# A hybrid DiT layer on one core: latents normalised tile by tile, gate rows loaded ahead of the down weights, router scaling split between ACT and GpSimd

## The reference, cut to what matters

```python
mod = silu(cond) @ w_ada + b_ada               # shift1, scale1, gate1, shift2, scale2, gate2
h   = rmsnorm(x, norm1) * (1 + scale1) + shift1
proj = h @ w_in                                # conv gates and values, cq 256, ckv 128, k_rope 32, merge gates
q   = rmsnorm(cq, q_norm) @ w_uq               # 8 heads x 96, 32 of them rotated
kv  = [rmsnorm(ckv, kv_norm), cache] @ w_ukv   # 8 heads x (64 + 64)
x   = x + gate1 * ((sig(g_conv) * conv + sig(g_mla) * attention) @ w_mix_out)
h2  = rmsnorm(x, norm2) * (1 + scale2) + shift2
route(h2 @ w_grp, h2 @ w_exp)                  # best of 4 groups, best 2 of its 8 experts
x   = x + gate2 * sum over experts(combine * (silu(h2 @ w_gate) * (h2 @ w_up)) @ w_down)
y   = rmsnorm(x, final_norm)
```

## Time and profile before

| | us |
|---|---|
| median of 3 runs (971.71 to 972.36) | 971.86 |
| the profiled execution, its own time | 970.25 |
| its span, first to last instruction | 968.4 |
| PE busy | 883.6 (91% of the span) |
| DVE, ACT, POOL busy | 411.7, 275.2, 106.6 |
| HBM traffic | 214 GB/s over the span |

### The profile page before, as it was taken

The page is one execution under the profiler, slowest core; times in us unless marked ns, Lnnn a source line. Parts: engine busy times, 40 slices in busy tenths (PEclk is TensorE's granted clock), DMA queues, the critical chain, the costliest instruction groups (busy, mean ns, idle before and its releaser), DMA issues.

```text
span 968.4 us, 14912 instructions
## 1 busy us (share of the span) xinstructions
PE 883.6 (91%) x6004; PEld 694.5 (72%) x6004; DVE 411.7 (43%) x854; ACT 275.2 (28%) x499; POOL 106.6 (11%) x121
## 2 busy tenths in 40 slices
PE   3698888999989999999999999994699999999886
PEld 2487546888789999999999997883355555555441
DVE  1437345444425234351521284568244334443232
ACT  5334835444421311212122132342011111111122
POOL 0000000000000000000000031001122332333220
PEclk9799998999999999999999999996799999999999
DMA  8951593112112122212222232797999999999938
GB/s 339 364 206 67 191 337 100 31 61 65 64 58 79 52 87 87 81 49 87 87 88 87 66 131 60 233 321 279 373 397 408 405 407 405 407 404 401 397 129 325
DMA packets 83919, 198.83 MB, mean 205 GB/s; under 512 B 11384, under 2 KB 43112, under 8 KB 83608
## 3 DMA queue, kind: packets, MB, share of 16 engines
q1 hardware_dynamic: 76040, 181.71, 51.0%
q0 software_dynamic: 7824, 16.36, 4.5%
HBM read 189.30 MB, written 18.17 MB: 214 GB/s over the span
## 4 chain that ended last, share of the span: by engine, by line
PE 79%; DMA 9%; DVE 4%; ACT 3%; SPq 3%; issue 1%; DVEq 0%; POOLq 0%; ACTq 0%
PE pair L798 12%; PE pair L1284 11%; PE pair L1288 11%; PE pair L1286 11%; PE pair L817 6%; PE pair L1277 5%; PE pair L1279 5%; PE pair L1278 5%; PE pair L1424 3%; PE pair L786 2%; DMA w_ug<-in_w_gate 2%; PE pair L1446 2%; PE pair L1436 2%; DMA ada_b<-in_w_ada 2%; DMA ya<-expert_rows 1%; DMA gate<-mod_rows 1%
## 5 line engine op out<-in xcount | busy, mean ns | idle before, releaser
L798 PE MATMUL pair<-w_ug,xgT 128*64 128x256 f32 x1184 | 141.9, 394 | 6.6 <-DMA w_ug<-in_w_gate 5.8
L1616 ACT CAST hi<-raw 128x2048 fp32r<-128x2048 f32 (+3 forms) x36 | 63.3, 1757 | 231.1 <-PE pair L1288 202.1
L1793 DVE TENSOR_TENSOR lo<-raw,hi 128x2048 fp32r<-128x2048 f32 (+3 forms) x36 | 78.5, 2181 | 118.5 <-ACT hi L1616 118.0
L798 PEld LDWEIGHTS pair<-w_ug,xgT 128*64 128x64 f32 x1184 | 85.4, 141 | 49.9 <-issue 8.2
L1288 PE MATMUL pair<-hT,lo 128*128 128x320 f32 x512 | 116.7, 309 | 0.0
L1284 PE MATMUL pair<-hT,hi 128*128 128x320 f32 x512 | 116.7, 309 | 0.0
L1286 PE MATMUL pair<-hT,hi 128*128 128x320 f32 x512 | 116.6, 309 | 0.0
L1284 PEld LDWEIGHTS pair<-hT,hi 128*128 128x128 f32 x512 | 85.6, 188 | 0.2 <-issue 0.2
L1288 PEld LDWEIGHTS pair<-hT,lo 128*128 128x128 f32 x512 | 85.6, 188 | 0.0
L1286 PEld LDWEIGHTS pair<-hT,hi 128*128 128x128 f32 x512 | 85.5, 188 | 0.0
L934 ACT ACTIVATE sa<-pair 64x256 f32<-64x256 f32 x37 | 14.1, 380 | 209.5 <-PE pair L798 209.5
(11 more groups left out here) (325 smaller groups left out, 1403.7 us busy)
## 6 DMA issues: line engine op xcount, KB each, us to landing
w_ug<-in_w_up SPq DMA_DIRECT2D x32, 1024.0 KB
w_ug<-in_w_gate SPq DMA_DIRECT2D x32, 1024.0 KB
w_dn<-in_w_down SPq DMA_DIRECT2D x32, 1024.0 KB
raw<-in_w_in SPq DMA_DIRECT2D x20, 1024.0 KB, 5.2
ada_a<-in_w_ada SPq DMA_DIRECT2D x16, 1024.0 KB, 10.0
ada_b<-in_w_ada SPq DMA_DIRECT2D x8, 1024.0 KB, 11.1
ya<-expert_rows SPq DMA_DIRECT2D x5, 1024.0 KB, 9.0
raw<-in_w_conv_out SPq DMA_DIRECT2D x4, 1024.0 KB, 5.0
```

The costliest lines, as they stand in the source:

```text
L798: x = pe.matmul(bank[2 + d % 2][g * SL:(g + 1) * SL, 0:DE], xgT[d % 2][:, k, h * SL:(h + 1) * SL], w_ug[r][:, g, h, k, :], start=(n == 0), ...
L1616: act.copy(hi[n % 2][:, 0:size], raw[n % 4][:, 0:size]).then_inc(hi_done, 1)
L1793: dve.tensor_sub(lo[n % 2][:, 0:size], raw[n % 4][:, 0:size], hi[n % 2][:, 0:size].bitcast(F32)).then_inc(lo_done, 1)
```

## The change

There are three groups of edits.

1. Latent stage. Roots and reciprocals are taken tile by tile, each tile with its own count (`s_rmsl`, `s_latn`), and PE transposes a tile after the count of that tile alone. Of the modulation pieces only 8 to 11 stay ahead of the transposes; 12 goes between the fourth and fifth tile, 13 to 15 between the key products (`ADA_KV`), all in bank 6. Pieces 14 and 15 load into `raw[0]` and `raw[1]`. The transposes go to banks 5, 0, 1, 2, 3, 4 with the rotary keys of the first four tiles in bank 7, the queries to (5, 0) and (1, 2), and `q_turn` has a single pair of banks (3, 4): each one now waits until ACT has copied the one before (`s_tqe`). Both halves of the `w_ukv` split stand later: DVE's behind the last query tile, ACT's behind the six rotary-key copies.
2. Last mix quarter and router. The +1 on scale2 is taken when the vector is made; the product with norm2 (1,024 columns for each stream) moves from one DVE instruction to two on GpSimd. `row_shift(3)` stands ahead of `add_y(1, 4)`. The four latent tiles' logits are scaled by ACT, in four small instructions behind the last `lg_out`, and DVE adds the shift to all four at once.
3. Gate rows. `gate2` lies elsewhere in SBUF; its four loads are issued as soon as the h2 rows are made, ahead of the downs of experts 1 and 2; DVE waits for them in step 1 only, where it first uses them.

```diff
 # SP
         sp.wait_ge(s_h2g, NT)
+        for st in range(2):
+            for h in range(2):
+                sp.dma_start(gate2[h * SL:(h + 1) * SL, st, :].rearrange("p (g c) -> p g c", g=2),
+                             MODW[3].rearrange("(g r) c -> g r c", g=4)[2 * h:2 * h + 2, st].partition_broadcast(SL)
+                             ).then_inc(s_g2, 16)
         sp.wait_ge(s_lg, NT)
...
         rows_stored(sp)
-        for st in range(2):
-            for h in range(2):
-                sp.dma_start(gate2[...
...
+                if q >= 14:
+                    sp.wait_ge(lo_done, q - 13)
+                    sp.wait_ge(ada_used, q - 5)
+                elif q == 13:
+                    sp.wait_ge(ada_used, 12)
+                elif q >= 6:
                     sp.wait_ge(ada_used, q - 5)
...
-        for q in range(12, N_ADA):
+        for q in (12, 14, 15, 13, *range(N_ADA2, N_ADA)):
             ada(q)
             if q == 19:
+                sp.wait_ge(ada_used, N_ADA2)
 # GpSimd
+        pool.wait_ge(s_n2, 48)
+        for st in range(2):
+            pool.tensor_mul(gain2[:, st, :], gain2[:, st, :], norm2_b[:, :]).then_inc(s_n2, 1)
 # ACT
+    def lg_scale(act, i):
+        act.wait_ge(s_lgT, i + 1)
+        act.wait_ge(s_h2g, i + 1)
+        act.activation(lg[:, i, :], lgT_of(i), ACT.Copy, scale=stat[:, 64 + i:65 + i]).then_inc(s_lge, 1)
...
         lg_out(act, NT - 1)
+        for i in range(NTS):
+            lg_scale(act, i)
...
-        for r, n in ((RQ, QL), (RKV, KVL)):
-            x = act.activation(stat[:, r:r + NT], stat[:, r:r + NT], ACT.Sqrt, scale=1.0 / n, bias=stat[:, 95:96])
-        x.then_inc(s_rmsl, 1)
-        act.wait_ge(s_ukv_v, 16)
-        split_hi(N_UKV, NH * P)
+            for r, n in ((RQ, QL), (RKV, KVL)):
+                x = act.activation(stat[:, r + i:r + i + 1], stat[:, r + i:r + i + 1], ACT.Sqrt, scale=1.0 / n,
+                                   bias=stat[:, 95:96])
+            x.then_inc(s_rmsl, 1)
 # PE
-        for q in range(N_ADA1, N_ADA2):
-            ada(q, bank[4 + q // 4][:, 0:256])
-        pe.wait_ge(s_latn, NT)
+        for q in range(N_ADA1, 12):
+            ada(q, bank[6][:, 0:256])
         for i in range(NT + 1):
...
+            if i == NTS:
+                pe.wait_ge(s_mod, 3)
+                ada(12, bank[6][:, 0:256])
+            if i < NT:
+                pe.wait_ge(s_latn, i + 1)
...
         def q_turn(i):
             pe.wait_ge(s_qr, i + 1)
-            if i < 2:
-                pe.wait_ge(s_kr, 2 * i + 4)
-            if i >= 2:
-                pe.wait_ge(s_tqe, i - 1)
+            if i == 0:
+                pe.wait_ge(s_lTe, NT + 1)
+                pe.wait_ge(s_kr, 4)
+            else:
+                pe.wait_ge(s_tqe, i)
...
+                if j in ADA_KV:
+                    ada(ADA_KV[j], bank[6][:, 0:256])
 # DVE
-        dve.wait_ge(s_rmsl, 1)
-        dve.reciprocal(stat[:, 32:37], stat[:, RQ:RQ + NT])
-        link(dve.reciprocal(stat[:, 37:42], stat[:, RKV:RKV + NT]))
         for i in range(NT):
             b = bank[i]
+            dve.wait_ge(s_rmsl, i + 1)
+            dve.reciprocal(stat[:, 32 + i:33 + i], stat[:, RQ + i:RQ + i + 1])
+            link(dve.reciprocal(stat[:, 37 + i:38 + i], stat[:, RKV + i:RKV + i + 1]))
...
-        dve.wait_ge(s_n2, 48)
-        link(dve.scalar_tensor_tensor(out=gain2[:, :, :], in0=gain2[:, :, :], scalar=1.0,
...
         row_gain(3)
+        row_shift(3)
         add_y(1, NT - 1)
-        row_shift(3)
         row_gain(4)
-        dve.wait_ge(s_lgT, 4)
-        for i in range(NT - 1):
-            lg_rows(i)
         row_shift(4)
+        dve.wait_ge(s_lge, NT + NTS)
+        link(dve.tensor_add(lg[:, 0:NTS, :], lg[:, 0:NTS, :], shift_bc[:, 0:1, :].to_broadcast([P, NTS, NG + NE])))
         dve.wait_ge(s_lgT, NT)
-        lg_rows(NT - 1)
+        lg_rows(NTS)
...
+            if isinstance(j0, int) and d == 1:
+                dve.wait_ge(s_g2, 64)
...
-        dve.wait_ge(s_g2, 64)
```

More of the change, by code:

```diff
@@ L412, in both, with kr_ps @@
         return pair[p][:, :].rearrange("p (h c) -> p h c", h=2)[:, :, 0:HALF]
+    def kr_ps(i):
+        if i < NTS:
+            return bank[7][0:ROPE, i * P:(i + 1) * P]
+        return bank[4][0:ROPE, 0:P] if i == NTS else bank[4][0:ROPE, 384:512]
     w_in = io["w_in"][0]
@@ L416, in build @@
     kcol = [0, 128, 256, 384, 640, 512]
+    lat_bank = [5, 0, 1, 2, 3, 4]
+    q_bank = [(5, 0), (1, 2)]
+    turn_bank = (3, 4)
+    kv_bank = (0, 1, 2, 5)
+    KR_ORDER = (0, 1, 4, 5, 2, 3)
+    ADA_KV = {1: 13, 3: 14, 5: 15}
     stream = [0, 0, 0, 0, 1]
@@ L443, in ada_buf @@
         if q < N_ADA2:
-            return ada_a[q % 6], ada_a_in[q % 6], 16 * (q // 6 + 1)
+            place = {13: ada_a[5], 14: v3(raw[0], 2, D), 15: v3(raw[1], 2, D)}.get(q, ada_a[q % 6])
+            return place, ada_a_in[q % 6], 16 * (q // 6 + 1)
         return ada_b[q % 4], ada_b_in[q % 4], 16 * ((q - N_ADA2) // 4 + 1)
@@ L1368, in q_of @@
         def q_of(i):
-            pe.wait_ge(s_lTe, i + 1)
-            if i == 1:
-                pe.wait_ge(s_kr, 2)
+            pe.wait_ge(s_lTe, 2 * i + 2 if i < 2 else i + 1)
             if i >= 2:
@@ L1381, in q_turn @@
             pe.wait_ge(s_qr, i + 1)
-            if i < 2:
-                pe.wait_ge(s_kr, 2 * i + 4)
-            if i >= 2:
-                pe.wait_ge(s_tqe, i - 1)
+            if i == 0:
+                pe.wait_ge(s_lTe, NT + 1)
+                pe.wait_ge(s_kr, 4)
+            else:
+                pe.wait_ge(s_tqe, i)
             for h in range(NH):
-                x = pe.transpose(bank[4 + 2 * (i % 2) + h // 4][0:QK, (h % 4) * P:(h % 4 + 1) * P],
+                x = pe.transpose(bank[turn_bank[h // 4]][0:QK, (h % 4) * P:(h % 4 + 1) * P],
                                  qtok[i % 2][:, h, :], ident)
@@ L1663, in _ @@
             act.copy(ckvT[0][:, kcol[i]:kcol[i] + P], b[:, 256:384]).then_inc(s_lTh, 1)
-        act.wait_ge(ada_used, N_ADA2)
-        for i in range(NT + 1):
-            act.wait_ge(s_lTe, i + 1)
+        act.wait_ge(ada_used, 13)
+        for i in KR_ORDER:
+            if i == NTS:
+                act.wait_ge(s_lTe, NT + 1)
             act.copy(kT[NOPE:QK, :, kcol[i]:kcol[i] + P],
-                     bank[2 + i][0:ROPE, 384:512].unsqueeze(1).to_broadcast([ROPE, NH, P])).then_inc(s_kr, 1)
+                     kr_ps(i).unsqueeze(1).to_broadcast([ROPE, NH, P])).then_inc(s_kr, 1)
+        act.wait_ge(s_ukv_v, 16)
+        split_hi(N_UKV, NH * P)
         for i in range(NT):
@@ L1685, in _ @@
             act.wait_ge(s_kv, j + 1) if kt < NKT else act.wait_ge(piece_used, N_UKV + 1)
-            act.copy(V[:, kt, :], bank[j % 4][:, :]).then_inc(s_kve, 1)
+            act.copy(V[:, kt, :], bank[kv_bank[j % 4]][:, :]).then_inc(s_kve, 1)
             j += 1
+            if kt == 0:
+                act.wait_ge(ada_used, N_ADA2)
+                act.copy(mod[1][:, :], bank[6][:, 0:256]).then_inc(s_mod, 1)
         def exps(n):
```

54 lines of the change are left out of this document (25 added, 29 removed).

## The result

The changed kernel takes **961.63 us** (median of 4 executions, 959.43 to 964.44) against 972.11 for the kernel before (971.71 to 972.75) on the same chip: ratio 0.9893, 95% interval 0.9865 to 0.9921, 10.5 us faster. The forecast was 963.1, with 957 to 967 as its range. The profiled execution of the changed kernel is the slowest of its four: 964.44, span 962.4.

What follows compares the result with a forecast made beforehand. Loads, not PE, were taken to end the expert stage. Latent 5.2 + mix and router 0.7 + gate rows 3.4 - clock 0.5 = 8.8 us off the profiled 970.25 gives 961.4, as a median 963.1; range 957 to 967.

Steps and rivals of the forecast that it cites:

- Latent stage, 5.2: Latent stage: first query tile 6.8 us earlier, less three losses, leaves 5.2 us gained; ends 3.0 and 6.8.
- (a): Latent stage: the second turn waits for ACT's rotary-key copies, `w_ukv` part and copy of turn 0; loses 0.3 us.
- (b): Latent stage: with one pair of banks the last turn waits for ACT's copy of turn 3; loses 1.0 us.
- (c): Latent stage: one modulation copy stands among ACT's value copies, which end the stage; loses 0.3 us.
- Mix and router, 0.7: End of the mix and router: DVE's last scaled logits come at 661.1 against 661.79, 0.7 us earlier.
- Gate rows, 3.4: Expert stage: moving the gate-row loads takes 1.3 us of bytes and a lull off the stream, 3.4 together; ends 1.3 and 8.4.
- Clock, -0.5: Expert stage: PE waits for more loads and a product may run slower; 0.5 us lost, ends 0 and 2.7.
- B: Expert stage: PE's earlier start counts in full, 8.4 us instead of 3.4 less 0.5; 957.6 us, chance 0.12.
- C: Latent stage: ACT paces turns and keys, so the gain is 2.0 us instead of 5.2; 966.3 us, chance 0.10.
- E: Expert stage: the gate rows do not leave the stream, 3.4 us becomes 0; 966.5 us, chance 0.05.
- D: Mix: GpSimd's product holds DVE, which is 4.5 us late; 967.6 us, chance 0.04.
- F: Expert stage: waits spread, the granted clock goes to 1.2 GHz and the kernel gets slower; 976.5 us with five steps, chance 0.03.

Runs made afterwards that it cites:

- e2: Kernel before with only DVE's wait for the gate rows moved behind the first step, loads left in their old place; 971.33 us, ratio 0.9994.
- e7: Changed kernel with ten extra 128x512 matmuls on PE ahead of the second expert's product; 965.02 us, ratio 0.9943 to the kernel before.
- e1: Kernel before with the move of the gate rows alone (buffer, loads and DVE's wait); 967.47 us against 971.51, ratio 0.9959.
- e3: Kernel before with the latent stage edits alone; 967.59 us, ratio 0.9948.
- e9: Kernel before with the mix and router edits alone; 970.96 us against 971.33, ratio 0.9994.
- e5: Changed kernel unaltered, timed again as a control; 961.01 us against 971.29 for the kernel before, ratio 0.9893.
- e10: Changed kernel with three more 128x1024 products on GpSimd, released with DVE's first gain row; 965.36 us, ratio 0.9919 to the kernel before.
- e11: Changed kernel with modulation piece 12 moved to ahead of the first turn; 961.27 us, ratio 0.9885 to the kernel before.
- e6: Changed kernel loading three quarters of the gate rows once more at their old place, in 384 pieces of 1 KB; 966.05 us, ratio 0.9937 to the kernel before.
- e12: Changed kernel with an extra 384 KB of weights loaded where the gate rows were, in 128 pieces of 3 KB; 964.28 us, ratio 0.9917 to the kernel before.

## Why the prediction was right, by its steps

**What bounds the kernel.** Right, and the step that decided: loads end the expert stage, so an idle PE in it is not worth its length. e2 gives PE 7.0 at the second product and gains nothing, e7 takes 8.85 from it and the stream loses 0.6.

**Latent stage, 5.2.** Measured 4.7 at the first scores against the trace of before, 5.5 on average against the four traces of the old stage. The first query copy gained 6.5 for 6.8. Of the losses, (a) was 0.3 at the second turn (3.31 after the first instead of 3.00), of which 0.2 was left at the last tile; (b), the wait of the last turn, was 0.9 for 1.0; (c), the copy among the values, 0.3 for 0.3. What the forecast had as covered and was not are the pieces among the key products: 0.4. That later stages "shift whole" is borne out within what the traces can tell. From the first scores to the `shift_bc` copy the four traces with the old stage take 520.2 to 521.6, and nine of the ten with the new one 520.3 to 521.9, so the 0.9 lost in the first pair of traces (520.9 and 521.8) is inside that scatter. The granted clock does not tell them apart either: over 120 to 180 the mean PEclk is 0.94 in the trace of before and 0.89 in the changed kernel's, but also 0.89 in e1 and e2, which have the old stage.

**Mix and router, 0.7.** Measured 0.76, and the steps came as summed: the first gain 0.9 sooner, the last `add_y` 4.04 earlier against 4.43 for the stage, the 0.4 foreseen, ACT's four scalings 0.84 in all, and DVE waiting for them. The logits were forecast near 655.9 and came at 656.6. GpSimd's product was 2.37, not 3.6. The Trainium skill (GPSIMD Engine Reference, section 3.1 Elementwise — side-by-side cycle accounting) has 4.5 us for an addition of 2,048 float32 columns, and the trace agrees with it: 4.75 for two products of 1,024.

**Gate rows, 3.4.** Measured 4.0 alone (e1; 2.6 to 5.3), and 4.1 in stream time: 255.1 to 256.0 in the four traces that have them in the stream (before, e2, e3, e9), 251.0 to 251.7 in the five that don't and have no other load (changed, e1, e5, e10, e11). The mechanism was right, bytes and a lull, and the lull was sized from two windows at 2.1 where it is about 2.7. The forecast put it down to "nothing but broadcast rows and few loads issued". The runs show the first half of this: e2, in which SP issued its next loads 7.5 earlier, kept the lull, and e6 brought it back with the pieces.

**Clock, -0.5.** Not borne out as a cost of the change. Beyond 3.67 the last product took 3.0, 0, 1.7, 1.4, 2.7, 2.7 and 1.7 in the seven traces that have all the edits and no filler there (changed, e5, e10, e11, e12, e6, e7), 1.9 on average, and 0, 2.7, 3.0, 1.7 and 2.75 in the other five (before, e1, e2, e3, e9), 2.0 on average. The trace of before, from which the term was reckoned, is the one of these five where it cost nothing. In single executions it went from nothing to 3.0, beyond the forecast's end of 2.7.

**The sum.** 8.8 forecast, 10.5 measured by the medians. The interval of the ratio (0.9865 to 0.9921) is 7.7 to 13.1 us, so the 1.7 between them is less than this timing can tell, and that the median came so near is in part luck. The profiled execution, forecast at 961.4, took 964.44, with its 3.0 for the clock at the end; that of e5, where the clock cost nothing, took 961.00. By the traces the gate term was some 0.6 short and the clock term 0.5 too much; the latent term depends on the trace that it is held against, from 0.8 too large to 1.6 too small.

**The rivals.** B fell to e2 and e7, C and E to e3 and e1. D's mechanism is real (e10, with another overlap than the one that D priced at 4.5, made DVE 2.5 late) and did not occur: `norm2_b` had landed at 630.40, so that both products were done 2.5 before the first gain. F did not occur: in the changed kernel's trace three products ran below full clock from 860 on (5.36, 5.36 and 6.65), and only the last had no load wait behind it to cover it.

## What to carry to other kernels

In a stage that ends on its loads, price an edit by what it takes off the stream and by when the stream starts; the longest wait of a compute engine in that stage can be worth nothing, and one run with only the wait moved shows it. Read the share of the DMA engines and their GB/s together: a share of 1.00 at 233 GB/s, where weights alone move 406, meant loads here that cost more than their bytes, and they belong in a place where the engines have room. Before a loss of under 1 us is put down to an edit, hold it against the same stretch in every trace that lacks the edit: here such stretches scatter by 1.4 to 2.3. Give such a stage's last wait a price of its own, because the product behind it, at half clock, stands uncovered at the end.
